# Expert weights of a mixture-of-experts stage: half of the pieces issued from ScalarE's DMA queue instead of all from SyncE's

## The reference

```python
D_MODEL, N_EXPERTS, TOP_K, D_FF_EXPERT, SEQ = 1024, 8, 2, 3584, 256

def swiglu(h, w1, w3, w2):
    return (jax.nn.silu(h @ w1) * (h @ w3)) @ w2

def moe_swiglu(h, router_w, router_b, w1, w3, w2):
    logits = (h @ router_w).astype(jnp.float32) + router_b.astype(jnp.float32)
    top_v, top_i = lax.top_k(logits, TOP_K)
    probs = jax.nn.softmax(top_v, axis=-1)
    combine = jnp.sum(jax.nn.one_hot(top_i, N_EXPERTS, dtype=jnp.float32) * probs[..., None], axis=-2)
    out = jnp.zeros_like(h)
    for e in range(N_EXPERTS):
        out = out + combine[..., e:e + 1].astype(h.dtype) * swiglu(h, w1[e], w3[e], w2[e])
    return out
```

## Time and profile before

| | |
|---|---|
| time, median of 3 runs | 2803.09 us (2799.95 to 2803.81) |
| the profiled execution | 2802.99 us, span 2801.2 us |
| granted TensorE clock over the span | 0.988 of full speed |
| TensorE matmul busy | 2734.2 us (98%) |
| VectorE, ScalarE, GpSimd busy | 1253.1, 597.5, 297.0 us |
| read from HBM | 629.76 MB |
| DMAs of expert weights | 1344 of 256 KB, all from SP |

### The profile page before, as it was taken

The page is one execution under the profiler, slowest core; times in us unless marked ns, Lnnn a source line. Parts: engine busy times, 40 slices in busy tenths (PEclk is TensorE's granted clock), DMA queues, the critical chain, the costliest instruction groups (busy, mean ns, idle before and its releaser), DMA issues.

```text
span 2801.2 us, 55963 instructions
## 1 busy us (share of the span) xinstructions
PE 2734.2 (98%) x22540; PEld 1884.1 (67%) x22540; DVE 1253.1 (45%) x2618; ACT 597.5 (21%) x1291; POOL 297.0 (11%) x490
## 2 busy tenths in 40 slices
PE   7999999999999999999999999999999999999999
PEld 5887899988876332323222232268879998878999
DVE  4555589744253023233231314254534752642674
ACT  3334444332242000100000000014331002351000
POOL 4000000000000222122212222103100000300000
PEclk9999999999999999999999999999999999999999
DMA  9455578842223999999999999954434554434542
GB/s 292 155 177 166 168 250 274 270 123 70 88 80 141 358 375 371 386 383 374 375 367 379 364 386 369 356 165 130 127 120 151 167 165 126 134 119 137 163 161 98
DMA packets 460994, 634.49 MB, mean 227 GB/s; under 512 B 29850, under 2 KB 278832, under 8 KB 460608
## 3 DMA queue, kind: packets, MB, share of 16 engines
q1 hardware_dynamic: 456896, 626.14, 65.2%
q10 hardware_dynamic: 1440, 3.52, 0.3%
q0 software_dynamic: 2400, 1.26, 0.2%
HBM read 629.76 MB, written 1.05 MB: 225 GB/s over the span
## 4 chain that ended last, share of the span: by engine, by line
PE 71%; SPq 19%; issue 5%; DMA 3%; DVE 1%; ACT 1%; ACTq 0%; DVEq 0%
PE bank L568 48%; PE accum L568 22%; SPq L3163 12%; SPq L3158 3%; SPq L3144 2%; DMA ring<-in_moe_w_dram 2%; DMA ring<-in_ada_w_dram 1%; SPq L3073 1%; DVE w L2088 1%; PE bank L689 1%; DMA w<-in_moe_w_dram 0%; PE accum L955 0%; PE bank L1208 0%; ACT L1557 0%; ACT sh L1557 0%
## 5 line engine op out<-in xcount | busy, mean ns | idle before, releaser
L568 PE MATMUL bank<-h,ring 128*128 128x256 f32 (+2 forms) x2272 | 455.1, 361 | 2.4 <-ACT h L1557 2.0
L568 PE MATMUL bank<-w 64*64 64x64 f32 (+5 forms) x5394 | 427.0, 317 | 4.9 <-ACT w L1661 2.3
L568 PEld LDWEIGHTS bank<-h,ring 128*128 128x128 f32 (+1 forms) x2272 | 391.0, 191 | 56.3 <-issue 9.9
L568 PEld LDWEIGHTS bank<-w 64*64 64x64 f32 (+3 forms) x5394 | 288.6, 143 | 136.4 <-issue 127.1
L568 PE MATMUL bank<-w,ring 128*128 128x256 f32 (+1 forms) x1660 | 304.1, 339 | 0.9 <-ACT w L1674 0.9
L568 PEld LDWEIGHTS bank<-w,ring 128*128 128x128 f32 x1660 | 268.1, 191 | 27.2 <-ACT w L1674 1.4
L568 PE MATMUL accum<-w 128*128 128x128 f32 (+6 forms) x2192 | 264.7, 387 | 0.2
L568 PE MATMUL bank<-ring,w 128*32 (+1 forms) x1742 | 240.9, 592 | 0.0
L568 PEld LDWEIGHTS accum<-w 128*128 128x128 f32 (+3 forms) x2192 | 184.6, 164 | 58.5 <-issue 50.3
L568 PE MATMUL accum<-h,ring 128*128 128x256 f32 (+2 forms) x1184 | 222.0, 342 | 0.0
L2088 DVE TENSOR_TENSOR w<-accum,w 128x512 f32<-128x512 f32 x108 | 74.7, 692 | 285.6 <-PE accum L568 278.7
(11 more groups left out here) (351 smaller groups left out, 3125.5 us busy)
## 6 DMA issues: line engine op xcount, KB each, us to landing
ring<-in_moe_w_dram SPq DMA_DIRECT2D x816, 256.0 KB, 6.7
w<-in_moe_w_dram SPq DMA_DIRECT2D x528, 256.0 KB, 6.8
ring<-in_w_in_dram SPq DMA_DIRECT2D x76, 1024.0 KB, 5.3
ring<-in_ada_w_dram SPq DMA_DIRECT2D x48, 1024.0 KB, 5.9
ring<-in_w_ffn_in_dram SPq DMA_DIRECT2D x44, 1024.0 KB, 5.1
ring<-in_ffn_w_dram SPq DMA_DIRECT2D x30, 1024.0 KB, 7.7
ring<-in_w_ffn_out_dram SPq DMA_DIRECT2D x16, 1024.0 KB, 5.1
ring<-in_w_o_dram SPq DMA_DIRECT2D x8, 1024.0 KB, 5.0
```

The costliest lines, as they stand in the source:

```text
L568: ins = nc.tensor.matmul(o, lhsT, rhs, start=start, stop=stop, skip_group_check=skip)
```

## The change

A piece n counts as ScalarE's where n is at least 5 and its k is odd (gate and up), or where k // 2 is odd (down: the pairs k = 2, 3 and k = 6, 7). SP skips those pieces and issues the others. ScalarE issues its pieces in its own program, in `load_behind(p)`, where n = p + 5: it waits until TensorE is done with piece p, then issues the eight DMAs (sixteen for a pair of a down phase). In each phase both engines read all eight numbers. 656 of the 1344 DMAs move to ScalarE.

```diff
+        def by_act(n):
+
+            kind, _, k = PIECES[n]
+            return n >= WIDE and (k // 2 if kind == "d" else k) % 2 == 1
...
+                    act.wait_ge(ids_ready, 1)
+                    expert = []
+
+                    def load_behind(p):
+
+                        n = p + WIDE
+                        if n >= len(PIECES):
+                            return
+                        kind, _, k = PIECES[n]
+                        if p == 0 or k == 0:
+                            expert[:] = [act.value_load(place_ids[0:1, r:r + 1], min_val=0, max_val=EXPERTS - 1)
+                                         for r in range(EXPERTS)]
+                        if not by_act(n):
+                            return
+                        act.wait_ge(wide_used[n % WIDE], n // WIDE)
+                        if kind == "d" and k % 2 == 0:
+                            return
+                        for r in range(EXPERTS):
+                            for to, src in expert_columns(n, expert[r]):
+                                act.dma_start(wide[to][:, r * WAYS:(r + 1) * WAYS], src.rearrange("o p n -> p (o n)")
+                                              ).then_inc(wide_loaded[to], 16)
...
+                        if k:
+                            load_behind(k - 1)
                     act.wait_ge(weighted, next_of("weighted"))
...
+                    for p, (kind, i, k) in enumerate(PIECES):
+                        if kind == "g" and k == KD - 1:
                             for j in range(NJ):
                                 act.wait_ge(*full(("eg", i, j)))
                                 fn(hid_e[:, j, :], psum_of(("eg", i, j)), ACT.Silu).then_inc(reader_of(("eg", i, j)), 1)
...
+                        if kind == "d" and i == CHUNKS_E - 1 and k == 0:
+                            for j in range(NJ):
+                                copy_hidden(i, j)
+                        if p >= KD - 1:
+                            load_behind(p)
+                        if kind == "g" and i and k in (1, 2, 3):
+                            copy_hidden(i - 1, 2 * k - 2)
+                            copy_hidden(i - 1, 2 * k - 1)
...
                     for n, (kind, i, k) in enumerate(PIECES):
-                        if k == 0:
-                            expert = [sp_.value_load(place_ids[0:1, r:r + 1], min_val=0, max_val=EXPERTS - 1)
-                                      for r in range(EXPERTS)]
+                        if n and k == 0:
+                            expert = [number(r) for r in range(EXPERTS)]
+                        if by_act(n):
+                            continue
```

More of the change, by code:

```diff
@@ L513, in table, with expert_columns @@
             return words(r * e).rearrange("p (r e) -> p r e", e=e)
+        def by_act(n):
+            kind, _, k = PIECES[n]
+            return n >= WIDE and (k // 2 if kind == "d" else k) % 2 == 1
+        def expert_columns(n, expert):
+            kind, i, k = PIECES[n]
+            if kind == "d":
+                row = i * FE + k // 2 * P
+                return [(to % WIDE, A["moe_w2"][0, bass.ds(expert, 1), row:row + P, col:col + WAYS])
+                        for to, col in ((n - 1, 0), (n, WAYS))]
+            w = A["moe_w1" if kind == "g" else "moe_w3"]
+            return [(n % WIDE, w[0, bass.ds(expert, 1), k * P:(k + 1) * P, i * FE:(i + 1) * FE])]
         def y_of(j):
@@ L1927, in _, with copy_hidden @@
                         fn(hgT[:, k, LATE:], t[:, NJ * STRIP:NDYN * STRIP], ACT.Copy).then_inc(reader_of(("dynamic", k)), 1)
+                        if k:
+                            load_behind(k - 1)
                     act.wait_ge(weighted, next_of("weighted"))
[L1929 to L1933, removed]
+                    def copy_hidden(i, j):
+                        act.wait_ge(*full(("eht", i, j)))
+                        fn(hidT(j, 0, FE), psum_of(("eht", i, j)), ACT.Copy).then_inc(reader_of(("eht", i, j)), 1)
+                    for p, (kind, i, k) in enumerate(PIECES):
+                        if kind == "g" and k == KD - 1:
                             for j in range(NJ):
@@ L1936, in _ @@
                                 fn(hid_e[:, j, :], psum_of(("eg", i, j)), ACT.Silu).then_inc(reader_of(("eg", i, j)), 1)
[L1937 to L1944, removed]
+                        if kind == "d" and i == CHUNKS_E - 1 and k == 0:
[6 more added lines that the diff above has]
+                            copy_hidden(i - 1, 2 * k - 1)
+                        if kind == "g" and i == 2 and k == KD - 1:
+                            for q in range(3):
+                                act.wait_ge(*full(("picks", q)))
+                                fn(pick_out[:, 2 * q:2 * q + 2, :], psum_of(("picks", q)).rearrange("p (j t) -> p j t", t=T),
+                                   ACT.Copy).then_inc(reader_of(("picks", q)), 1)
             table_of_roots()
@@ L3141, in _, with number @@
                     sp_.wait_ge(ids_ready, next_of("ids_ready"))
+                    def number(r):
+                        return sp_.value_load(place_ids[0:1, r:r + 1], min_val=0, max_val=EXPERTS - 1)
+                    expert = [number(r) for r in range(EXPERTS)]
                     for n, (kind, i, k) in enumerate(PIECES):
-                        if k == 0:
-                            expert = [sp_.value_load(place_ids[0:1, r:r + 1], min_val=0, max_val=EXPERTS - 1)
-                                      for r in range(EXPERTS)]
+                        if n and k == 0:
+                            expert = [number(r) for r in range(EXPERTS)]
+                        if by_act(n):
+                            continue
                         if n < SLOTS // 2:
```

## The result

| | before | after |
|---|---|---|
| median | 2801.8 us (4 runs, 2799.95 to 2803.81) | 2870.02 us (4 runs, 2868.36 to 2872.65) |
| ratio | | 1.0246, 95% interval 1.0233 to 1.0259 |
| profiled execution | 2802.99 us, clock 0.988 | 2872.65 us, span 2870.6, clock 0.977 |

The change costs 68 us. The forecast was 2872 (69 more), slower with a chance of 0.86.

The account below looks back on a forecast made before the run. Transfers and TensorE run almost level, transfers slightly slower; delays over some 4 us per period make TensorE the bound. Added 8.0 up to d0, 53 over five periods and 7.9 to d6: 69 on 2802.99, 2872 us; range 2815 to 2895, likeliest 2850 to 2885.

Parts of the forecast that it names:

- The Silus behind sixteen DMAs: Before each down phase: ScalarE's pair k = 2, 3 delays the first Silu; down starts 10.1 us after last gate piece's start.
- rival three: Issuing from ScalarE is slower, 0.63 us per DMA instead of 0.51, giving 2891 us; chance 0.14.
- The slow clock: After TensorE's idle times before down and at k = 6: clock at 0.50, 2.8 us more charged each time.
- Pair k = 4, 5 and the stall at k = 6: Down phase: k = 4 starts at 24.1 us; first up piece shares engines, k = 6 lands 5.4 later, starting at 40.3.
- Rival one: Sharing between the two queues costs nothing; each of six down phases is 8.2 us shorter, 2823 us; chance 0.17.
- rows 10: Profile rows at program start: SP's five 1 MB loads took 14.0 us each, ScalarE's 9.4; cited for queues sharing engines.
- The copies: Gate phases from g1: eight DMAs ahead of two copies on ScalarE make TensorE's transposes lose 0.8 us per phase.
- What was costed at nothing: 168 reads of numbers on ScalarE, and those on SP, taken as hidden; uncovered ahead of a Silu, some 3 us per phase.
- The period and the sum: Gate, down and up take 145.0 us instead of 134.4, five periods 53 more; with 8.0 and 7.9, 69 us in all.
- Rival two: SP's issuing gaps were the bound; a period falls to 130.4 us, 4.0 less, six times: 2779 us; chance 0.09.
- Rival four: Sharing is harmless and two thirds of the stalls fall into waits already there: no change; chance 0.05.
- less than 386 GB/s in up phases: Sign of a right forecast in the profile after: DMA engines move less than 386 GB/s in up phases.

Follow-up runs that it names:

- the two parts alone: Kernel before, with ScalarE issuing only down pair k = 2, 3: 2835.99 us; or only the first up piece of chunks 1 to 6: 2818.48 us.
- by one queue or two: Kernel before, numbers read early on SP: 2795.35 us; changed kernel with down pairs exchanged between engines, copies first, numbers early: 2796.48 us.

## Why the prediction was right

**The Silus behind sixteen DMAs.** Predicted 10.1 us from the start of the last gate piece to the down phase, measured 10.30 (1468.04 to 1478.34). The burst took 8.25 us against 8.08 taken from SP, and rival three (0.63 us per DMA on ScalarE, 10.1 for the burst) is refuted. The first Silu of g0, behind eight DMAs and the table load, was to cost 2.2 and cost 2.1 in the ledger. Undoing the part with the sixteen DMAs gave 43 us back. What the prediction missed here is d1: the copies of the picks behind the Silus were in no term. From d0 to d1 takes 147.6 us (1045.30 to 1192.92), the other four steps 143.3 in the mean; before, it was 134.0 and 134.5.

**The slow clock.** TensorE's granted clock was 0.50, the 1.2 GHz level, behind the idle 4.97 us, and the first down piece took 8.02 us (7.95 predicted). At k = 6, behind 5.53 idle, the piece took 6.97 (1518.02 to 1524.99), not 7.95. This term was 1.0 too large; with 0.6 on the start of k = 6 (below) it is the difference between a down phase of 51.8 us (1478.34 to 1530.14) and the 53.4 predicted. Over the six phases I estimate 2.5 us in the mean for the restart at the down phase and 1.8 at k = 6, as half of the time that TensorE worked at the low level; 2.8 was charged for each. The last section shows why the two differ.

**Pair k = 4, 5 and the stall at k = 6.** Predicted at 24.1 and 40.3 after the phase's start; measured 23.6 and 39.7. Rival one (the sharing costs nothing, 2823) is refuted by the queues' rows and by the holding back of the up piece. The price was right, but rows 10, on which it leaned, show less than the prediction took from them. The 14.0 us is a median of five loads that also wait behind one another in SP's queue (by the trace they land at 6.03, 13.43, 16.87, 19.94 and 23.10), so they show that ScalarE's load did not wait its turn behind them, and not in what shares two queues divide the engines. That is shown first by the changed kernel: 852 against 844 packets in the same 8 us. The Trainium skill (DMA: Bandwidth & Descriptors, section Queues, rings and completion order) states that the engines take turns between queues by packets; the rows agree.

**The copies.** Predicted 0.8 per gate phase; the ledger's "gate" goes from 25.1 to 30.1, 0.8 in each of six, and returns to 25.1 where the copies stand first.

**What was costed at nothing.** The reads of the numbers: in the ledger the first three up pieces have no excess in the changed kernel, as before.

**The period and the sum.** The period was predicted at 145.0 and measured at 144.1; five of them are 48.7 us more than before, not 53. Up to d0 the change costs 8.7 (predicted 8.0; from the start of the first gate piece), from d5 to d6 6.4 (7.9), and behind the start of d6 2.0 ("within 1"). That the sum, 69, is level with the 69.7 of the profiled executions is in part luck: 4.3 us too much in the five periods (too much for the clock at k = 6, nothing for the picks) and 1.5 in the step to d6 are made good by 0.7 more up to d0, the 2.0 behind the start of d6 and the 4 us of scatter outside the stage.

**The other rivals.** **Rival two** (SP's gaps were the bound, 2779) is refuted as a size: with the gaps gone, by one queue or two, 6 to 7 us were to be had, not 24. **Rival four** (no change) is refuted by the 68 us.

**Off:** I had named less than 386 GB/s in up phases as a sign of a right forecast. It was 385, which is no difference. The transfers lose their time in the down phases (335 GB/s over the phase), not in the up phases. And the two parts alone sum to 50 us of 68, the copies to 5 more by the ledger: each part alone can hide behind the waits for transfers that were there before (28.1 into the down phases), and that cover is used only once. I argue this from the ledger; no run isolates it.

## What to carry to other kernels

A share of the chain in an issuing queue is not yet a bound. Here it was 58.6% between 1400 and 1600 us, with the DMA engines at a share of 1.04 to 1.05, and removing SP's gaps gave 6 to 7 us of 2801: look at the windows' GB/s before adding an issuer. Put issues on a compute engine only behind what others wait for, since a burst of sixteen held its next instruction for 8.25 us. Between the two queues no order was kept (1518.77 against 1518.74 for pieces issued 5.3 us apart), so pieces that are needed in turn must be issued in turn across both, and when one overtaking is removed, ask which engine is late next.

## What was not expected of the hardware

- A piece issued 5.3 us later in the other queue landed level with the pair ahead of it (1518.77 against 1518.74), with 385 GB/s moved in all.
- ScalarE issues a DMA as fast as SP does: sixteen in 8.25 us against 8.08.
- While both queues had work, each moved half of the packets (852 and 844 in 8 us), whichever had been issued first.
- The slow clock was charged differently behind idle times of about the same length (4.97 and 5.53 us): the pieces took 8.02 and 6.97 us. The record of the granted clock shows why. Windows of the changed kernel over the low level at the first down piece and the rest of that piece, and the same for k = 6:

```profile
1477.29:1484.12 6.83, 5.78 (x28) 1.60 (x32) 1.75 (x3) 3.04 (x6) 1.18 (x2) 0.50 0.92 340
1484.12:1486.36 2.24, 2.24 (x25) 0.68 (x21) 1.62 (x3) 0.00 (x0) 0.00 (x0) 1.00 0.04 13
1514.84:1521.67 6.83, 3.65 (x20) 0.99 (x24) 0.69 (x1) 0.00 (x0) 2.35 (x4) 0.50 1.05 387
1521.67:1524.99 3.32, 3.32 (x34) 0.84 (x29) 2.69 (x4) 0.00 (x0) 0.00 (x0) 1.00 1.06 387
```

The granted clock was 0.50 for 6.83 us in both, and 1.00 behind it. What differed is how much of that fell into TensorE's idle time: 1.05 us in the first (1477.29 to the restart at 1478.34), 3.18 in the second (1514.84 to 1518.02). So TensorE worked 5.78 and 3.65 us at the low level. The clock had fallen 3.9 us after TensorE stopped in the first case and 2.4 us after it in the second; why at these moments I leave open. The second row also shows the engines at 13 GB/s: there the transfers lose their time, since the four down pieces have landed by 1485.13 and SP issues the next pair only at 1487.59, once TensorE is done with the first.
